# Silu as one ScalarE function in place of tanh and a VectorE product, in a two-layer gated DeltaNet and convolution trunk

## What is computed

```python
def hybrid_mixer(h, w_in, ...):
    proj = h @ w_in
    qkv, g_out, a, b, glu, gates = jnp.split(proj, bounds, axis=-1)
    qkv = jax.nn.silu(causal_depthwise_conv(qkv, qkv_conv_w))      # width 4
    q = l2norm(q.reshape(shp)) * (HEAD_DIM_DN ** -0.5)
    k = l2norm(k.reshape(shp))
    o = gated_delta_chunked(q, k, v, g, beta)                      # 8 heads of 128
    o = rmsnorm(o, head_norm) * jax.nn.silu(g_out...)
    y_a = o.reshape(...) @ w_a_out
    c = val * jax.nn.sigmoid(gt)
    c = causal_depthwise_conv(c, dw_conv_w) + dw_conv_b            # width 31
    c = jax.nn.silu(rmsnorm(c, conv_norm))
    y_b = c @ w_b_out
    merged = jax.nn.sigmoid(gate_a) * y_a + jax.nn.sigmoid(gate_b) * y_b
    return merged @ w_o
```

## Time and profile before

| | us |
|---|---|
| median of three runs (2691.64 to 2691.96) | 2691.8 |
| the profiled execution | 2693.1 |
| its span, first to last instruction | 2691.3 |
| TensorE matmul busy | 2670.0 |
| VectorE busy | 1597.9 |
| ScalarE busy | 1100.4 |
| GpSimd busy | 255.7 |

### The profile page before, as it was taken

One profiled execution on the slowest core, in us unless ns is written; L12 is line 12 of the kernel. 1 busy time (PEld: TensorE's weight loads), 2 busy tenths in 40 slices (PEclk: granted clock), 3 DMA queues, 4 the chain that ended last, 5 costly groups with the idle time before them and its releaser, 6 DMA issues.

```text
span 2691.3 us, 35214 instructions
## 1 busy us (share of the span) xinstructions
PE 2670.0 (99%) x12744; PEld 2220.5 (83%) x12744; DVE 1597.9 (59%) x2697; ACT 1100.4 (41%) x1817; POOL 255.7 (9%) x231
## 2 busy tenths in 40 slices
PE   9999999999999999999999999999999999999998
PEld 7888878888878888888888888788888788888887
DVE  6554358999985345554355543689998843455532
ACT  4222247767653332222222223477676523322222
POOL 0000022122220010000000000222212100100000
PEclk9999999999999999999999999999999999999999
DMA  5233336565543323333322333455556333233331
GB/s 168 94 100 97 99 97 144 121 157 126 135 116 100 96 86 102 97 99 94 102 95 94 96 92 101 109 140 125 139 121 152 94 111 100 90 97 94 97 95 66
DMA packets 83480, 291.87 MB, mean 108 GB/s; under 512 B 10032, under 2 KB 10800, under 8 KB 83376
## 3 DMA queue, kind: packets, MB, share of 16 engines
q1 hardware_dynamic: 68112, 235.72, 27.9%
q0 software_dynamic: 14976, 54.53, 10.8%
q10 hardware_dynamic: 288, 0.27, 0.0%
HBM read 233.86 MB, written 2.10 MB: 88 GB/s over the span
## 4 chain that ended last, share of the span: by engine, by line
PE 95%; DVE 3%; issue 1%; ACT 0%; DMA 0%; DVEq 0%; SPq 0%; POOLq 0%; POOL 0%
PE bank L461 94%; DVE cacc L1572 1%; PE bank L660 1%; PE bank L708 1%; DVE X L1681 1%; DVE X L1684 0%; DVE bank L1687 0%; ACT X L1106 0%; DMA xT<-in_x 0%; DVE X L1676 0%; PE bank L481 0%; DVE h_lo L1299 0%; DVE hf L1596 0%; DVE c_all L1575 0%; DVE y L1374 0%
## 5 line engine op out<-in xcount | busy, mean ns | idle before, releaser
L1274 DVE TENSOR_TENSOR w_lo<-raw,w_hi 128x1024 fp32r<-128x1024 f32 x342 | 422.7, 1237 | 535.6 <-ACT w_hi L874 535.4
L874 ACT ACTIVATE w_hi<-raw 128x1024 fp32r<-128x1024 f32 x446 | 469.5, 1054 | 651.2 <-PE bank L461 651.1
L461 PE MATMUL bank<-h_hi,w_hi 128*128 128x512 f32 x1504 | 587.4, 391 | 1.6 <-issue 1.2
L461 PE MATMUL bank<-h_hi,w_lo 128*128 128x512 f32 x1504 | 585.5, 389 | 0.0
L461 PE MATMUL bank<-h_lo,w_hi 128*128 128x512 f32 x1504 | 585.3, 389 | 0.0
L461 PE MATMUL bank<-g_hi,w_lo 128*128 128x512 f32 x928 | 380.6, 410 | 0.0
L461 PE MATMUL bank<-g_hi,w_hi 128*128 128x512 f32 x928 | 378.1, 407 | 0.0
L461 PE MATMUL bank<-g_lo,w_hi 128*128 128x512 f32 x928 | 369.2, 398 | 0.0
L1572 DVE SCALAR_TENSOR_TENSOR cacc<-c_raw,ncol,cacc 128x512 f32<-128x512 f32 x464 | 334.0, 744 | 2.6 <-ACT cacc L1124 2.2
L461 PEld LDWEIGHTS bank<-h_hi,w_hi 128*128 128x128 f32 x1504 | 282.3, 188 | 63.3 <-issue 2.8
L461 PEld LDWEIGHTS bank<-h_hi,w_lo 128*128 128x128 f32 x1504 | 282.3, 188 | 59.1
(11 more groups left out here) (260 smaller groups left out, 3275.2 us busy)
## 6 DMA issues: line engine op xcount, KB each, us to landing
raw<-in_w_in SPq DMA_DIRECT2D x128, 512.0 KB, 3.8
w_lo<-raw POOLq DMA_DIRECT2D x104, 512.0 KB, 5.2
raw<-in_ffn_w_up SPq DMA_DIRECT2D x88, 512.0 KB, 3.6
raw<-in_ffn_w_gate SPq DMA_DIRECT2D x87, 512.0 KB, 3.5
raw<-in_ffn_w_down SPq DMA_DIRECT2D x64, 512.0 KB, 3.5
raw<-in_ffn_w_down SPq DMA_DIRECT2D x32, 384.0 KB, 3.1
raw<-in_w_a_out SPq DMA_DIRECT2D x16, 512.0 KB, 3.6
raw<-in_w_b_out SPq DMA_DIRECT2D x16, 512.0 KB, 3.9
```

The lines of the kernel that those rows point to most:

```text
L461: return nc.tensor.matmul(o, a, b, start=start, stop=stop, **kw)
L874: nc.scalar.activation(w_hi[c % SLOTS][:, :], raw[c % SLOTS][:, :], ACT.Copy).then_inc(hi_done, 1)
L1274: tt(w_lo[c % SLOTS][:, :], raw[c % SLOTS][:, :], w_hi[c % SLOTS][:, :].bitcast(F32), ALU.subtract).then_inc(lo_v, 1)
```

## The change

ScalarE makes silu(2x) as one function, Silu with scale 2.0, directly from ka, qa, va into kT, qT, va, and from hb into cth. VectorE's 48 products on q, k, v and 16 on the convolution go. kT is now written at the end of the round before, so that instruction waits for TensorE's step p3 of that round, which reads the old kT, where the tanh waited for xtf; qT waits for ScalarE's own square of the old qT. The two last stages of the convolution's norm (c_hi, c_lo) read cth, which has two buffers, so that each silu from the third on waits for the c_lo two before. A one-column exponential into a tile of its own (`first`, L1133) stands ahead of the wait for kt.

```diff
-DVE_STEPS = ["hs", "kT", "qT", "dmin", "skE", "rden", "bnk2", "neg", "NT", "vT", "diag", "cin", "own"]
+DVE_STEPS = ["hs", "dmin", "skE", "rden", "bnk2", "neg", "NT", "diag", "cin", "own"]
...
-ACT_STEPS = ["thk", "thq", "thv", "ksq", "eg", "decT", "kd", "near"]
+ACT_STEPS = ["kT", "qT", "vT", "ksq", "eg", "decT", "kd", "near"]
...
                     elif name == "kt":
-                        ve("kT")
+                        ac("kT")
                         turn(bank[1], kT, name)
...
                     elif name == "kq":
-                        ve("qT")
+                        ac("qT")
                         each(bank[3], kT, qT, name)
                     elif name == "vt":
-                        ve("vT")
+                        ac("vT")
...
                 def silu_halves(rd):
-                    act.wait_ge(pe_dn.sem, pe_dn.after(rd - 1, "xtf"))
+                    act.wait_ge(pe_dn.sem, pe_dn.after(rd - 1, f"p{NC - 1}"))
                     act.wait_ge(ve_ds.sem, ve_ds.after(rd, "k3"))
-                    nc.scalar.activation(Y[:, :], ka[:, :], ACT.Tanh).then_inc(*ac_dn.step("thk"))
-                    nc.scalar.activation(X[:, :], qa[:, :], ACT.Tanh).then_inc(*ac_dn.step("thq"))
+                    nc.scalar.activation(kT[:, :], ka[:, :], ACT.Silu, scale=2.0).then_inc(*ac_dn.step("kT"))
+                    act.wait_ge(ac_dn.sem, ac_dn.after(rd - 1, "qsq"))
+                    nc.scalar.activation(qT[:, :], qa[:, :], ACT.Silu, scale=2.0).then_inc(*ac_dn.step("qT"))
                 def front(rn):
                     act.wait_ge(ve_ds.sem, ve_ds.after(rn, "v3"))
-                    nc.scalar.activation(thv[:, :], va[:, :], ACT.Tanh).then_inc(*ac_dn.step("thv"))
+                    nc.scalar.activation(va[:, :], va[:, :], ACT.Silu, scale=2.0).then_inc(*ac_dn.step("vT"))
...
+                    nc.scalar.activation(first[:, :], pw[:, 0, 0:1], ACT.Exp)
                     pe_("kt")
...
                     hi(*held)
-                    ve("vT")
                     odd_columns(4)
...
-                def c_tanh(k):
+                def c_silu(k):
                     act.wait_ge(cn_done, l * 8 + (k + 1))
                     if k >= 2:
-                        act.wait_ge(cp_done, l * 8 + (k - 1))
-                    nc.scalar.activation(cth[k % 2][:, :], hb[k % 4][:, :], ACT.Tanh).then_inc(cth_done, 1)
+                        act.wait_ge(clo_v, l * 8 + (k - 1))
+                    nc.scalar.activation(cth[k % 2][:, :], hb[k % 4][:, :], ACT.Silu, scale=2.0).then_inc(cth_done, 1)
...
-                    act.wait_ge(cp_done, l * 8 + (k + 1))
-                    nc.scalar.activation(c_hi[:, k, :], hb[k % 4][:, :], ACT.Copy).then_inc(chi_done, 1)
+                    act.wait_ge(cth_done, l * 8 + (k + 1))
+                    nc.scalar.activation(c_hi[:, k, :], cth[k % 2][:, :], ACT.Copy).then_inc(chi_done, 1)
...
-                        def act_of(n, src, dst, th):
-                            ac(f"th{n}")
-                            stt(out=dst[:, :], in0=th[:, :], scalar=1.0, in1=src[:, :], op0=ALU.add, op1=ALU.mult).then_inc(*ve_dn.step(f"{n}T"))
-                        act_of("k", ka, kT, Y)
-                        act_of("q", qa, qT, X)
                         late_tap()
...
-                        act_of("v", va, va, thv)
                         near_blocks()
...
-                def c_silu(k):
-                    dve.wait_ge(cth_done, l * 8 + (k + 1))
-                    stt(out=hb[k % 4][:, :], in0=cth[k % 2][:, :], scalar=1.0, in1=hb[k % 4][:, :], op0=ALU.add, op1=ALU.mult).then_inc(cp_done, 1)
                 def c_rest(k):
                     dve.wait_ge(chi_done, l * 8 + (k + 1))
-                    tt(c_lo[:, k, :], hb[k % 4][:, :], c_hi[:, k, :].bitcast(F32), ALU.subtract).then_inc(clo_v, 1)
+                    tt(c_lo[:, k, :], cth[k % 2][:, :], c_hi[:, k, :].bitcast(F32), ALU.subtract).then_inc(clo_v, 1)
```

More of the change, by code:

```diff
@@ L159, in trunk @@
         pw = sb("pw", [2, NC])
+        first = sb("first", [1])
         hnw = sb("hnw", [1])
@@ L292, in trunk @@
         cn_done = sem("cn_done")
-        cp_done = sem("cp_done")
         ab_h = sem("ab_h")
@@ L1014, in dense_steps @@
                         if t == 0:
-                            act.wait_ge(ve_dn.sem, ve_dn.after(l * 8 + 7, "vT"))
+                            act.wait_ge(ac_dn.sem, ac_dn.after(l * 8 + 7, "vT"))
                             act.wait_ge(pe_dn.sem, pe_dn.after(l * 8 + 7, "vt"))
@@ L1022, in dense_steps @@
                         nc.scalar.activation(dst[:, SC - 1:], bk[:, :], ACT.Copy).then_inc(*ac_ds.step(f"{n}_raw"))
-                        act.wait_ge(ve_dn.sem, ve_dn.after(rd - 1, f"{n}T"))
+                        act.wait_ge(ac_dn.sem, ac_dn.after(rd - 1, f"{n}T"))
                         if n == "v":
@@ L1214, in _ @@
                 head((Rt, 0, None), l * 8 + 7, (Rh + 9, 15))
-                def c_tanh(k):
+                def c_silu(k):
                     act.wait_ge(cn_done, l * 8 + (k + 1))
                     if k >= 2:
-                        act.wait_ge(cp_done, l * 8 + (k - 1))
-                    nc.scalar.activation(cth[k % 2][:, :], hb[k % 4][:, :], ACT.Tanh).then_inc(cth_done, 1)
-                c_tanh(0)
+                        act.wait_ge(clo_v, l * 8 + (k - 1))
+                    nc.scalar.activation(cth[k % 2][:, :], hb[k % 4][:, :], ACT.Silu, scale=2.0).then_inc(cth_done, 1)
+                c_silu(0)
                 for k in range(KT):
                     if k < KT - 1:
-                        c_tanh(k + 1)
-                    act.wait_ge(cp_done, l * 8 + (k + 1))
-                    nc.scalar.activation(c_hi[:, k, :], hb[k % 4][:, :], ACT.Copy).then_inc(chi_done, 1)
+                        c_silu(k + 1)
+                    act.wait_ge(cth_done, l * 8 + (k + 1))
+                    nc.scalar.activation(c_hi[:, k, :], cth[k % 2][:, :], ACT.Copy).then_inc(chi_done, 1)
                     if k == 1:
@@ L1804, in c_norm @@
                     if k >= 4:
-                        dve.wait_ge(clo_v, l * 8 + (k - 3))
+                        dve.wait_ge(cth_done, l * 8 + (k - 3))
                     stt(out=hb[k % 4][:, :], in0=c_all[:, k, :], scalar=pcol[:, k, PR_CN:PR_CN + 1], in1=bank[6][:, :],
                         op0=ALU.mult, op1=ALU.mult).then_inc(cn_done, 1)
-                def c_silu(k):
-                    dve.wait_ge(cth_done, l * 8 + (k + 1))
-                    stt(out=hb[k % 4][:, :], in0=cth[k % 2][:, :], scalar=1.0, in1=hb[k % 4][:, :], op0=ALU.add, op1=ALU.mult).then_inc(cp_done, 1)
                 def c_rest(k):
                     dve.wait_ge(chi_done, l * 8 + (k + 1))
-                    tt(c_lo[:, k, :], hb[k % 4][:, :], c_hi[:, k, :].bitcast(F32), ALU.subtract).then_inc(clo_v, 1)
+                    tt(c_lo[:, k, :], cth[k % 2][:, :], c_hi[:, k, :].bitcast(F32), ALU.subtract).then_inc(clo_v, 1)
                 def gated(n):
@@ L1832, in _ @@
                 for k in range(KT):
-                    if k < KT - 1:
-                        c_silu(k)
                     if k + 2 < KT:
                         c_norm(k + 2)
-                    elif k == KT - 2:
-                        c_silu(KT - 1)
                     c_rest(k)
```

## The result

The changed kernel takes 2702.7 us (median of 5 runs, 2702.6 to 2704.7), the kernel before in the same series 2691.8 (5 runs, 2691.6 to 2693.6): 1.0041 times as long, with a 95% interval of 1.0030 to 1.0052. That is 10.9 us slower, where 9.9 were forecast. The profiled execution took 2704.1 us.

The account below looks back on a forecast made before the run. TensorE, with matmuls busy 2670.0 of 2691.3 us, was taken as the bound. The median 2691.8 plus 9.9 (6.6 for two first heads, 3.3 for one clock fall, other parts 0) gave 2701.7 us; range 2697 to 2708.

Parts of the forecast that it names:

- A load costs its row and the lost overlap: ScalarE table load between back-to-back instructions: delays the second by 1.28 + 0.02 + 0.1 = 1.4 us, no drain.
- Part 1: VectorE's 64 products go, 44 us of its work; TensorE's waits of 7.4 us and 4.2 us per layer stay.
- Part 2: Two loads per later round: vs 0.25 us late, 0.2 us of slack left at step rows, cost 0.
- Part 3: Four loads in each layer's first head: TensorE 3.3 us later, +6.6 us for two layers.
- Part 4: TensorE's clock after the new first-head stalls: one fall in the two, +3.3 us, bounds 0 and 6.6.
- Part 5: Convolution's norm: one load per layer in an idle stretch of ScalarE, TensorE does not wait, cost 0.
- a load costs twice: Rival: ScalarE empties and refills for about as long again at each load; 2728 us, chance 0.06.
- VectorE is the bound: Rival: VectorE's freed time reaches its chain ends, waits shrink and the clock stays up; 2680.4 us, chance 0.04.
- the first head hides it: Rival: first-head loads run beside other work, nothing is left; about 2692 us, chance 0.12 for hidden or half hidden.
- the clock staying up after one stall or after both: First-head clock falls: one 2701.7 us, chance 0.40; none 2698.4, 0.22; the rival with both falling 2705.0, 0.16.

Follow-up runs that it names:

- without the first heads' loads: Changed kernel with both first heads in the old form (tanh on ScalarE, product on VectorE), no table loads there: 2692.0 us, ratio 0.9997.
- the tap move: Two late convolution taps put earlier on VectorE: changed kernel with old first heads 2685.8 us, kernel before 2705.9, changed kernel 2694.4.
- Some 0.55 us more of delay: Changed kernel with old first heads, plus five more one-column exponentials ahead of vs in the 14 later rounds: 2695.7 us, ratio 1.0011.
- the load without cover: Changed kernel without the one-column exponential, so the table load comes ahead of qd's exponential: 2713.0 us, ratio 1.0075.
- the loads alone: Kernel before plus three one-column functions in each first head that force the same loads; tanh and products stay: 2701.2 us, ratio 1.0031.
- the convolution's norm alone: Kernel before with Silu replacing tanh and product only in the convolution's norm, one load per layer: 2692.9 us, ratio 1.0003.

## Why the prediction held

The total was right, 2701.7 forecast and 2702.7 measured, and so were its parts except one, which came out right in the sum by luck.

- **A load costs its row and the lost overlap, 1.4 us.** Right: 42 loads with a mean of 1283 ns, the next instruction 0.01 to 0.02 us behind. By the Trainium skill, page "ScalarE: Activation LUTs", section "What ACT_TABLE_LOAD costs", each switch costs about 1380 ns of drain besides the load; in the rows above three loads with their work take 410.10 to 416.55, which leaves no room for one.
- **Part 1, the products are worth nothing on the path.** Right: the waits of 8.4 and 7.4 us stayed (7.8 in the changed trace), and without the first heads' loads the ratio is 0.9997. What I did not see is that they were worth something to another edit: with the tap move it is 2685.8 without them and 2705.9 with them.
- **Part 2, the later rounds' loads are hidden with 0.2 us to spare.** Right at step rows. vs starts as soon as `first` allows, NT waits 0.28 us for dec's exponential, `own` ends at 564.81, the hand-over takes 0.06 and TensorE comes at 565.06: 0.19 us left. Some 0.55 us more of delay showed as 0.34 us of waiting and 0.21 of time per round, the load without cover as about 0.8.
- **Part 3, 3.3 us per first head.** Right: 3.4 and 3.4. The wait for hs came to 1.28 us (0.38 + 0.93 = 1.31 forecast), those for kT and va vanished, and the stall at rows was 3.17 where 3.3 was said. Together 6.8 for 6.6.
- **Part 4, one fall of the clock for 3.3 us.** The step that failed, in both of its numbers. Both stalls brought the clock down in the profiled execution, and each lower stretch cost 1.5 or 1.6 us instead of 3.3. I had taken the 3.3 us from the 9.2 us behind the end of the heads; behind the new stalls the lower stretch was half as long, 3.4 us instead of 6.8. Two halves are one whole, and so the sum (3.1) was right for a wrong reason. That it is luck is seen in the kernels with the loads alone and with the moved taps, where one stall of the two was followed by no fall.
- **Part 5, the convolution's norm is free.** Right: 1.0003.
- The remaining 1.2 us were in no term of the sum: 0.7 is the place of an old fall of the clock, 0.5 the longer wait ahead of xt2 in one round of each layer, both told above, and 0.1 was there before the first heads part.

Of the rivals, "a load costs twice" (2728), "VectorE is the bound" (2680) and "the first head hides it" (2692) are excluded by the runs above. With the clock staying up after one stall or after both, the time would be lower by 1.5 or 3; the kernel with the loads alone had such a stall in its first layer, and whether the runs of the changed kernel at 2702.6 and those at 2704.7 differ by this was not measured.

## What to carry to other kernels

A function from another table costs its load where ScalarE's instructions stand back to back with something the bound engine waits for, and nothing where idle time and slack cover it (here 1.15 us of idle time, and 0.2 us of slack left behind it); a one-column dummy function chooses which of the two it is (10 us here), and the rare first round, where other functions split the run of one table, needs its own look. Work taken off an engine that isn't the bound is worth nothing by itself: it is room, and is worth what can be moved into it (7 to 8 us here; against the kernel before 6.6 are left, and only without the first heads' loads). Before moving work forward in a queue, count the slack to every step that waits behind it, not only to the one in mind, and look at what the other engines do at the new place: one instruction took 1.77 us there instead of 0.74.

## What the hardware did unexpectedly

The same idle time of TensorE does not always cost the same clock. Around the 4.2 us of waiting at the end of the heads the records of the ten traces show the lower clock for 6.8 us in 14 cases and for 3.4 us in 6 (both times in the kernels with the convolution's norm alone and without the small exponential). Behind stalls of 3.0 to 3.2 us it was 3.4 us, or, in the first layers of the kernels with the loads alone and with the moved taps in the changed one, none at all; the fourteen waits of 1.6 us in the kernel before with the moved taps never brought it down. What decides between these cases is not shown. One such fall is worth 1.5 to 3.3 us of 2700, which is as much as the runs of one kernel spread (2690.6 to 2694.0 for the kernel before): a theory that differs from its rival by 2 us has to be read in the waits, and not in the total.

The same instruction of VectorE can more than double in time by where it lands: a convolution tap took 1.77 us instead of 0.74 in each of the 14 rounds in which it started under GpSimd's sum into attn.
